# One transformer block with product-key experts: gates placed by a scattering DMA that adds, and 768 columns of the second expert table taken by gathered rows for half of the tokens

## The reference, cut to what matters

```python
q = einsum('bsd,de->bse', x, wq).reshape(B, S, 8, 2, 128)
s1 = einsum('bshc,kc->bshk', q[..., 0, :], keys1)     # 8 heads x 128 scores
s2 = einsum('bshc,kc->bshk', q[..., 1, :], keys2)
v1, i1 = top_k(s1, 16);  v2, i2 = top_k(s2, 16)
cand = v1[..., :, None] + v2[..., None, :]            # 16 x 16 candidates
vals, pos = top_k(cand, 16)                           # 16 experts of a head
ids = i1[pos // 16] * 128 + i2[pos % 16]              # expert out of 128 x 128
gates = softmax(vals)
# per token: 8 heads x 16 = 128 experts
h = einsum('td,tkd->tk', x, u_tab[ids])
a = gelu(h) * gates
f = einsum('tk,tkd->td', a, v_tab[ids])               # v_tab: 16384 x 2048
```

## Time and profile before

| | us |
|---|---|
| median of 3 runs (2413.35 to 2413.64) | 2413.36 |
| the profiled execution | 2416.51 |
| span of its trace | 2414.8 |
| PE busy | 2307.8 (96%) |
| DVE busy | 1538.1 (64%) |
| ACT busy | 1028.5 (43%) |
| POOL busy | 72.5 (3%) |

### The profile page before, as it was taken

The page is one execution under the profiler, slowest core; times in us unless marked ns, Lnnn a source line. Parts: engine busy times, 40 slices in busy tenths (PEclk is TensorE's granted clock), DMA queues, the critical chain, the costliest instruction groups (busy, mean ns, idle before and its releaser), DMA issues.

```text
span 2414.8 us, 45807 instructions
## 1 busy us (share of the span) xinstructions
PE 2307.8 (96%) x15504; PEld 2135.9 (88%) x15504; DVE 1538.1 (64%) x2726; ACT 1028.5 (43%) x1390; POOL 72.5 (3%) x64
## 2 busy tenths in 40 slices
PE   4999999899899989999999999999999999999996
PEld 4999999897699879999999999999788888888885
DVE  4446655565653568777779898989555555555556
ACT  2444455554444443444443333333444444444442
POOL 0000000000010040000000000000000000000000
PEclk9999999999999999999999999999999999999998
DMA  6655555455544555555554445444566666666663
GB/s 178 189 182 164 172 178 168 155 181 177 192 142 156 187 166 172 182 182 182 181 177 131 160 157 159 157 157 157 182 193 194 202 205 201 201 202 202 206 193 123
DMA packets 116576, 425.28 MB, mean 176 GB/s; under 512 B 13840, under 2 KB 13856, under 8 KB 115520
## 3 DMA queue, kind: packets, MB, share of 16 engines
q1 hardware_dynamic: 112608, 412.14, 54.1%
q0 software_dynamic: 3936, 12.71, 2.2%
HBM read 418.50 MB, written 6.29 MB: 176 GB/s over the span
## 4 chain that ended last, share of the span: by engine, by line
PE 90%; DVE 5%; DMA 3%; issue 1%; ACT 1%; DVEq 0%; SPq 0%; ACTq 0%
PE ps L1212 24%; PE ps L1199 17%; PE ps L1194 17%; PE ps L1195 17%; PE ps L1219 12%; PE ps L1448 2%; DMA raw<-in_w_in 2%; DVE w_lo L720 1%; DMA ln_gb<-in_ln_in 1%; DVE bn L733 0%; DVE x L739 0%; DVE tk_ab L1022 0%; PE ps L1320 0%; PE ps L1390 0%; DVE x L745 0%
## 5 line engine op out<-in xcount | busy, mean ns | idle before, releaser
L720 DVE TENSOR_TENSOR w_lo<-raw,w_hi 128x1024 fp32r<-128x1024 f32 x774 | 957.7, 1239 | 713.7 <-PE ps L1219 418.0
L436 ACT ACTIVATE w_hi<-raw 128x1024 fp32r<-128x1024 f32 x774 | 820.5, 1061 | 1061.2 <-DMA raw<-in_peer_v 384.2
L1194 PE MATMUL ps<-x_t_hi,w_hi 128*128 128x256 f32 x3328 | 835.9, 289 | 21.0 <-ACT v_t L486 12.5
L1195 PE MATMUL ps<-x_t_lo,w_hi 128*128 128x256 f32 x3328 | 820.9, 284 | 0.0
L1194 PEld LDWEIGHTS ps<-x_t_hi,w_hi 128*128 128x128 f32 x3328 | 641.7, 193 | 25.9 <-ACT w_hi L436 15.9
L1195 PEld LDWEIGHTS ps<-x_t_lo,w_hi 128*128 128x128 f32 x3328 | 642.4, 193 | 0.0
L1199 PE MATMUL ps<-x_t_hi,w_lo 128*128 128x256 f32 x3328 | 472.1, 285 | 13.5 <-DVE w_lo L720 13.5
L1199 PEld LDWEIGHTS ps<-x_t_hi,w_lo 128*128 128x128 f32 x3328 | 433.3, 194 | 14.8 <-DVE w_lo L720 14.7
L1212 PE MATMUL ps<-w_hi,x_t_hi 128*128 128x512 f32 x1024 | 315.8, 390 | 3.0 <-DVE x_t_lo L1131 3.0
L1212 PE MATMUL ps<-w_hi,x_t_lo 128*128 128x512 f32 x1024 | 316.1, 390 | 0.0
L1219 PE MATMUL ps<-w_lo,x_t_hi 128*128 128x512 f32 x1024 | 274.1, 389 | 0.0
(11 more groups left out here) (204 smaller groups left out, 1313.8 us busy)
## 6 DMA issues: line engine op xcount, KB each, us to landing
raw<-in_u SPq DMA_DIRECT2D x256, 512.0 KB, 4.6
raw<-in_peer_v SPq DMA_DIRECT2D x256, 512.0 KB, 4.9
raw<-in_w_in SPq DMA_DIRECT2D x128, 512.0 KB, 4.6
raw<-in_branch SPq DMA_DIRECT2D x32, 512.0 KB, 3.9
raw<-in_wout SPq DMA_DIRECT2D x32, 512.0 KB, 3.7
raw<-in_wq SPq DMA_DIRECT2D x32, 512.0 KB, 3.8
raw<-in_pleg SPq DMA_DIRECT2D x32, 512.0 KB, 3.8
x<-in_x SPq DMA_DIRECT2D x2, 1024.0 KB, 6.2
```

What stands on the lines that cost most here:

```text
L436: nc.scalar.activation(HI[:, u % 4, :], RAW[:, u % 4, :], ACT.Copy).then_inc(hi_ready, 1)
L720: v.tensor_tensor(LO[:, u % 2, :], RAW[:, u % 4, :], HI[:, u % 4, :].bitcast(F32), ALU.subtract) \
L1194: mm(o, w(HI, u % 4)[:, k, :], xh[:, ks * half + k, :], start=(s and k == 0), stop=False)
L1195: mm(o, w(HI, u % 4)[:, k, :], xl[:, ks * half + k, :], start=False, stop=False)
```

## The change

It does five things.

1. **Search.** The stages are rewritten as `tk0` to `tk15`, each for both token tiles of one head, and DVE runs them one a unit from unit 7 of `wq` through all of `pleg` to unit 70 of `u`. The last stage writes for each pick the number of its cell in a matrix [128 chunks, 128 experts, 128 tokens] (`ID`) and, for the second token tile, the number of its row in the table (`IDV`).
2. **Gates.** Two such matrices stand in DRAM (`gates_dram`, one a token tile). POOL fills them with zeros by 16 DMAs of 1 MB in pieces of 512 bytes, issued when phase `v` is done; DVE's first pooling sum (`pool_sums`) waits for them, because their source shares its memory. After the spill POOL issues 256 indirect DMAs that add one gate in each of 128 cells, in three batches of heads as the softmax is ready (DVE units 6, 40, 82 of `u`). From DVE's unit 151 of `u` on, `gated(k)` multiplies chunk k of `BUF` by its gates, which POOL has loaded by two DMAs a chunk into one of three slots. One-hot rows, gate products, `spread` and both memsets are gone.
3. **Hidden values.** ACT also writes each finished chunk of the second token tile to DRAM (`hidden`, 64 KB) after gelu.
4. **Second table.** In the odd units of `vtab` PE makes only 256 of the 1024 columns for the second token tile. The other 768 are made row by row: for each of the 128 picks of a token POOL gathers the hidden value (128 cells of 4 bytes) and the row piece (128 rows of 3072 bytes, seven slots), and DVE adds value times row to `ACC` (`pick`), one pick a chunk or a little more, from chunk 10 on.
5. **Order.** DVE's programs of `wq`, `pleg`, `u` and `vtab` are written out instead of looped.

```diff
+            pool.wait_ge(zero_ready, 1)
+            pool.wait_ge(unit_done, BASE["qk"])
+            for n in range(16):
+                pool.dma_start(gates_dram[n // 8][n % 8 * 16:n % 8 * 16 + 16].rearrange("k p e -> p k e"), ZERO[:, :, :]
+                               ).then_inc(zero_out, 16)
...
-            pool.wait_ge(spill_out, 32)
-            nc.gpsimd.memset(BUF[:, TOPK_CHUNKS:FIRST_ONES, :], 1.0).then_inc(ones_ready, 1)
-            pool.wait_ge(picks_sb, 1)
-            nc.gpsimd.memset(BUF[:, FIRST_ONES:NK, :], 1.0).then_inc(ones_ready, 1)
...
+                        for p in range(TOPK * h, TOPK * (h + 1)):
+                            pool.indirect_dma_start(out=cells[tt], out_offset=bass.IndirectOffsetOnAxis(
+                                ap=ID[:, tt, p:p + 1], axis=0), in_=GATE[:, tt, p:p + 1], in_offset=None,
+                                compute_op=ALU.add).then_inc(scattered[tt], 16)
...
+            for p in range(PICKS):
+                if p >= ROWS:
+                    pool.wait_ge(row_used, p - ROWS + 1)
+                pool.indirect_dma_start(out=ROW[p % ROWS][:, :], out_offset=None, in_=table,
+                                        in_offset=bass.IndirectOffsetOnAxis(ap=IDV[:, p:p + 1], axis=0)
+                                        ).then_inc(row_in[p % ROWS], 16)
+                if p + TOPK < PICKS:
+                    picked(p + TOPK)
...
             def pool_sums(g):
-                dve.wait_ge(const_ready, 3)
+                dve.wait_ge(const_ready, 4)
+                dve.wait_ge(zero_out, 16 * 16)
...
+            def gated(k):
+
+                dve.wait_ge(h_out[k % 4], 16 * (k // 4 + 1))
+                dve.wait_ge(g_in[k % G_SLOTS], 16 * NT * (k // G_SLOTS + 1))
+                v.tensor_tensor(BUF[:, k, :], BUF[:, k, :], GR[:, k % G_SLOTS, :], ALU.mult).then_inc(g_mult, 1)
+
+            st = stage("pleg", KD + 2, gt_block, AH, AL)
+            for n in range(32):
+                conv(None, 4, BASE["wq"] + n + DVE_LEAD)
+                search(n - 7)
+            for n in range(32):
+                if n % 2 == 0:
+                    st(None, n // 2)
+                conv(None, 4, BASE["pleg"] + n + DVE_LEAD)
+                search(25 + n)
+            done = 0
+            for n in range(2 * NK):
+                conv(None, 4, BASE["u"] + n + DVE_LEAD)
+                search(57 + n)
+                for b, at_unit in enumerate((6, 40, 82)):
+                    if n == at_unit:
+                        gates_out(b)
+                while done < min((n - G_FROM) * 5 // 4, n // 2 - 2):
+                    gated(done)
+                    done += 1
+            for k in range(done, NK):
+                gated(k)
...
+                    dve.wait_ge(row_used, p)
+                    ins = v.scalar_tensor_tensor(out=ACC[:, :], in0=ROW[p % ROWS][:, :], scalar=HP[:, p:p + 1],
+                                                 in1=ACC[:, :], op0=ALU.mult, op1=ALU.add)
...
+                def pieces(tt):
+                    if u >= BASE["vtab"] and half and tt:
+                        return [(q, min(512, REST - 512 * q)) for q in range(2) if REST > 512 * q]
+                    return [(0, 512), (1, 512)]
```

More of the change, by code:

```diff
@@ L50 @@
 DVE_LEAD = 1
-TOPK_CHUNKS = 64
-FIRST_ONES = 104
+PICKS = HEADS * TOPK
+BATCHES = ((0, 3), (3, 5), (5, 8))
+STAGES = 16
+ROUND = 1.5 * 2.0 ** 23
+G_SLOTS = 3
+GC = 768
+DC = D - GC
+REST = DC - UNIT
+ROWS = 7
+PICKS_FROM = 10
+G_FROM = 150
 def t5_buckets():
@@ new lines, in _ @@
+            for tt in range(NT):
+                pool.wait_ge(scattered[tt], 16 * PICKS)
+            for k in range(NK):
+                if k >= G_SLOTS:
+                    pool.wait_ge(g_mult, k - G_SLOTS + 1)
+                for tt in range(NT):
+                    pool.dma_start(GR[:, k % G_SLOTS, tt * P:(tt + 1) * P], gates_dram[tt][k]
+                                   ).then_inc(g_in[k % G_SLOTS], 16)
+            hidden_cells = hidden.rearrange("k p t -> (k p t)").unsqueeze(1)
+            table = a["peer_v"].rearrange("a b (c d) -> (a b c) d", d=256)
@@ new lines, in _, with picked @@
+            for n in range(4):
+                pool.wait_ge(h_out[n], 16 * NK // 4)
+            def picked(p):
+                pool.indirect_dma_start(out=HP[:, p:p + 1], out_offset=None, in_=hidden_cells,
+                                        in_offset=bass.IndirectOffsetOnAxis(ap=ID[:, 1, p:p + 1], axis=0)
+                                        ).then_inc(h_in[p // TOPK % 2], 16)
+            for p in range(TOPK):
+                picked(p)
+            pool.wait_ge(unit_done, BASE["vtab"])
@@ L666, in gelu_b @@
-            def gelu_b(i):
-                for j in range(4):
-                    conv(i, 4, BASE["u"] + 2 * TOPK_CHUNKS + j + ACT_LEAD)
-                    if j % 2:
-                        act.wait_ge(unit_done, val(i, 4, BASE["u"] + 2 * TOPK_CHUNKS + j + 1))
-                        ps = PS[:, 2 * (j // 2), 0:S]
-                        nc.scalar.activation(ps, ps, ACT.Gelu).then_inc(gelu_ready, 1)
-            with act.Fori(0, 32) as i:
-                gelu_b(i)
+            run("u", 32, 8, gelus, start=8, stop=10)
@@ L678, in _ @@
+            exp_gates(2)
+            run("u", 32, 8, gelus, start=10, stop=20)
+            act.wait_ge(ids_ready, HEADS)
+            run("u", 32, 8, gelus, start=20)
             vb = BASE["vtab"]
@@ L966, in _ @@
             xt_lo(1)
-            run("wq", 8, 4, {})
-            run("pleg", 8, 4, {}, pre=stage("pleg", KD + 2, gt_block, AH, AL))
             def settle():
@@ new lines, in _, with tk0, tk1 @@
+            scores = lambda h, tt, f: SC[:, 2 * h + tt, f, :]
+            first = lambda h: slice(TOPK * h, TOPK * h + 8)
+            second = lambda h: slice(TOPK * h + 8, TOPK * (h + 1))
+            def tk0(h):
+                dve.wait_ge(peer_sb, h + 1)
+                for tt, f in each:
+                    ch.tag(v.max(V16[:, tt, f, 0:8], scores(h, tt, f)))
+                settle()
+            def tk1(h):
+                for tt, f in each:
+                    ch.tag(v.max_index(IU[:, tt, f, 0:8], V16[:, tt, f, 0:8], scores(h, tt, f)))
@@ L1101, in _ @@
-            dve.wait_ge(act_evac, 80 + TOPK_CHUNKS)
-            onehots(None, 0)
-            onehots(None, 1)
-            conv(None, 4, ub + 3)
-            onehots(None, 2)
-            spread(None, 0)
-            conv(None, 4, ub + 4)
-            onehots(None, 3)
-            onehots(None, 4)
-            spread(None, 1)
-            def u_body(i, last):
-                for j in range(4):
-                    if not (last and j == 3):
-                        onehots(i, j + 1)
-                    conv(i, 4, ub + j + DVE_LEAD)
-                    if j % 2:
-                        spread(i, j // 2)
@@ L1210, in his @@
                         for s, stn in enumerate((ah, al)):
-                            for q in range(2):
-                                mm(nbank(tt, 2 * half + q), stn[:, tt * P:(tt + 1) * P],
-                                   HI[:, u % 4, q * 512:(q + 1) * 512], start=(first and s == 0), stop=False,
+                            for q, w in pieces(tt):
+                                mm(nbank(tt, 2 * half + q)[:, 0:w], stn[:, tt * P:(tt + 1) * P],
+                                   HI[:, u % 4, q * 512:q * 512 + w], start=(first and s == 0), stop=False,
                                    skip_group_check=True)
@@ L1217, in los @@
                     for tt in range(NT):
-                        for q in range(2):
-                            r = mm(nbank(tt, 2 * half + q), ah[:, tt * P:(tt + 1) * P],
-                                   LO[:, u % 2, q * 512:(q + 1) * 512], start=False, stop=last,
+                        for q, w in pieces(tt):
+                            r = mm(nbank(tt, 2 * half + q)[:, 0:w], ah[:, tt * P:(tt + 1) * P],
+                                   LO[:, u % 2, q * 512:q * 512 + w], start=False, stop=last,
                                    skip_group_check=True)
```

406 lines of the change are left out of this document (200 added, 206 removed).

## The result

The changed kernel takes 2452.5 us (median of 4 runs, 2447.6 to 2453.7), the kernel before 2413.5 (4 runs, 2413.35 to 2413.86): a ratio of 1.0158, 95% interval 1.014 to 1.0175. I had forecast 2229 and a gain. The time is 223 us above the forecast and 132 above the top of its range (2320), and the direction is wrong too: the loss is small, but clear of the noise.

A forecast was written before the change was run, and what follows sets the result against it. PE was taken to set the pace nearly everywhere: 2414.8 - 127.8 - 64.9 - 5.4 + 8 + 3.5 + 0.9 - 0.9 = 2228.2, with 2 for first landings 2230.2, forecast 2229 us. The sum's own range was 2216 to 2250, the overall range 2214 to 2320.

The forecast's parts named there:

- rival 1: POOL's indirect DMAs too slow: scatters above 1.62 us stall `u`, gathers above 2.22 `vtab`; 2.28 cancels the gain; chance 0.09.
- Rival 2: POOL and DVE block each other: indirect DMAs hold DVE in `vtab`; at 0.53 us each, 2303 us; chance 0.10.
- Second table on PE, -127.8: `vtab`: fewer PE columns cut a chunk from 5.436 to 4.437 us, for 128 chunks -127.8 us.
- rival 3: `vtab`: DMA engines get full, landing grows beyond 6.3 us; at 7 us 118 chunks cost 43, 2272 us; chance 0.14.
- 4: `vtab`: the table's own stream is at its limit; if it can't pass 200 GB/s, 103 us, 2332; chance 0.06.
- Second half of `u`, -64.9: Without gate products its 128 units go at the first half's pace, 368.1 for 432.96 us: -64.9 us.
- Zero fill, +8: 16.8 MB of zeros between `v` and the first pooling sum: from hidden to 22 us late, taken as +8.
- rival 5: Zero fill late before the first pooling sum: at 45 GB/s PE stands for 264 us, 2485; chance 0.06.
- `pleg`, +3.5: Low part behind a `conv` and a search stage: PE waits 0.2 us at each of 16 chunks, +3.5 (0 to 9).
- First memset, -5.4: POOL's first memset goes, and with it PE's 5.41 us of standing for the next low part: -5.4 us.
- End of `u`, +0.9: Last chunk's gelu, DRAM write, `gated` and `a_lo` take 3.9 us where PE stood 3.02 before: +0.9 us.
- Very end, -0.9: After PE's last unit DVE adds 256 columns where it added 1024: -0.9 us.

The follow-up runs named there:

- second experiment: Changed kernel with the 256 scatters writing in place of adding; 2568.4 us (one run).
- third: Changed kernel with DVE's subtraction in units 4 to 255 of `u` taking its second operand from PSUM, unrelated numbers of the same size; 2319.9 us.
- fifth experiment: Changed kernel with ACT also converting table blocks into PSUM for DVE's subtraction (units 10 to 255 of `u`), first gate product at unit 175; 2260.3 us, ratio 0.936.
- short rows: Changed kernel with gathered rows cut to 256 of 768 columns, which DVE reads three times; 2432.9 us.
- fourth experiment: Changed kernel with gate products from unit 246 of `u` (before: 150), most of them in `vtab`, and gathered rows from chunk 40 (before: 10); 2363.6 us, ratio 0.978.

## Why the prediction was wrong

**The step that failed** is the price of an indirect DMA on POOL, and with it the weight of rival 1. I took 1.1 to 1.6 us, "nearer the plain issue" of 0.53, and gave the rival 0.09. For the gathers that was right (1.22 + 0.30 = 1.52); an adding scatter cost 2.39. The sum put it at nothing, hidden behind `u`, and it was 197 us. The rival's own arithmetic was right: from 905.7 to 1517.5, 256 scatters at a mean of 2.39 us, against 1.62 that the kernel could bear, make 197 us, and PE stood for 197. It had the place (unit 151) and the mechanism (DVE waits with all conversions behind it). What it lacked were two additions that no row of before showed: the adding form (0.6 us on 0.96, second experiment) and the wait for DVE's two-operand conversions (up to 1.04 more, third and fifth experiment). The second half of the rival, gathers at a limit of 2.22, did not come: 1.22 + 0.30, and POOL waited 208 us for DVE.

**Rival 2 was the clue, read in one direction.** I had the rows that show DVE and POOL in each other's way (`conv` 4.28 beside an addition) and asked only what POOL does to DVE. For indirect DMAs, gathers too, it is the other way round: DVE's conversion keeps its 1.23 and POOL's instruction waits. Put into rival 1, 1.54 + 1.04 + 0.30 = 2.88 is over its deciding 2.28.

**Term by term.** Second table on PE, -127.8: PE's side as forecast, but 34 us came back. From 1825.13 to 2427.4 `vtab` lasted 602.3 us for 568 (against the trace of before, where it lasts 698.2, 95.9 are won and 31.9 missing); 20 of it is rival 3 (DMA share 0.92, landing 6.0), below the 43 that I had priced, and 14 not settled. Rivals 2 (as put) and 4 did not come: DVE's conversions stay at 1.22 to 1.24, and the short rows let the table's stream pass 235 GB/s (1.049 MB in 4.46 us). Second half of `u`, -64.9: right in pace. Zero fill, +8: nothing; 371 GB/s at a share of 1.01, then 320, with PE at 419 and 421 matmuls in 50 us, and no idle time near 200. The spill's row was the right one to take, rival 5's the wrong one. `pleg`, +3.5: 3.9, from PE's idle time at 776.7 in the trace of before and 773.4 after, to 871.4 and 872.0 at the end of it. First memset, -5.4: the first half of `u` takes 380.8 us for 387.3, -6.5, but that is partly luck. The 5.41 us are gone; where PE had stood 2.40 and 2.27 it now stands 7.45, for the search has two of its little steps beside POOL's additions, where I had written that this place is "left as it is"; and PE comes out of one such halt at half its clock in place of three (granted 0.94 for 0.91 from 870 to 960). End of `u`, +0.9: 4.53 for 3.02, +1.5. Very end, -0.9: +2.0, from PE's last unit to the end of the span 24.0 us for 22.0, without a cause that I can name. Among the chances, the mild halves of rivals 1, 2 and 5 add up to 0.15 by their own figures and not to 0.11; nothing hangs on it.

**The account**: 2228.2 forecast, + 197.2 for the stall, + 2.6 for the rest of `u`'s second half (PE came out of the stall at a granted clock of 0.5, which costs about 1.6), + 31.9 in `vtab`, + 0.6 at the end of `u`, + 2.9 at the very end, - 1.1 for the first half of `u`, + 0.4 for `pleg`, - 8 for the zero fill make 2454.7; PE stood 3.3 us ahead of the trace of before at 773 us already, without a cause in the change that I can name. That gives 2451.4, which is the span.

## What to carry to other kernels

An instruction that no row prices needs a bound worked from what stands behind it: here 1.62 us was known, and a price of "1.1 to 1.6, nearer 0.53" was a hope. Where work is put on an idle engine, ask both ways who holds whom: count on the engine that was idle being the one that is stretched. And where a chain of small things must end before a fixed place in a queue, its start, its rate and that place belong together; make the rate (one SBUF operand taken out of DVE's conversions, 133 us), move the place (25 units later, most of the other 60 of the 192), or both; and where much is moved, as in the fourth experiment, see that the ring behind it is long enough and that what follows isn't crowded.
